# A routed expert stage: down weights in two buffers by parity, blank slots not gathered, router weights stationary in four column groups

## What is computed

```python
pg = softmax(xf @ w_rg); g_top = argmax(pg); pg_top = max(pg)
fl = (xf @ w_re) of the group g_top                   # 4 logits
top_p, top_i = top_k(softmax(fl), 2)
wts = top_p / sum(top_p) * pg_top
act = silu(xf @ w_gate[e]) * (xf @ w_up[e]) * comb[e] # comb: wts, 0 for experts not chosen
y = sum over e of act @ w_down[e]
```

## Time and profile before

| what | value |
|---|---|
| median of three runs | 2178.8 us (2172.47 to 2181.87) |
| profiled execution | 2173.51 us |
| its span, first to last instruction | 2171.4 us |
| PE busy | 1713.8 us, 79% |
| mean granted clock of TensorE | 0.831 |
| bytes by DMA | 375.76 MB |

### The profile page before, as it was taken

The page is one execution under the profiler, slowest core; times in us unless marked ns, Lnnn a source line. Parts: engine busy times, 40 slices in busy tenths (PEclk is TensorE's granted clock), DMA queues, the critical chain, the costliest instruction groups (busy, mean ns, idle before and its releaser), DMA issues. The chain is left out here.

```text
span 2171.4 us, 18914 instructions
## 1 busy us (share of the span) xinstructions
PE 1713.8 (79%) x7209; PEld 961.2 (44%) x7209; DVE 410.9 (19%) x828; ACT 283.2 (13%) x561; POOL 73.4 (3%) x96
## 2 busy tenths in 40 slices
PE   4699999937997588889769967786577878788781
PEld 2254444435555355677644435755323323233230
DVE  1110000031222343333340023112200000010104
ACT  1100000042221122222210011001000000000001
POOL 0000000000000000000000000000010010011010
PEclk9899999967997699855579979686687888798885
DMA  5354424043310445100052260027499699969984
GB/s 223 121 205 185 152 80 155 8 148 119 116 49 1 145 125 154 51 1 0 10 204 78 77 232 0 1 78 263 164 402 395 251 394 407 395 247 409 391 321 167
DMA packets 112001, 375.76 MB, mean 173 GB/s; under 512 B 18750, under 2 KB 46310, under 8 KB 82162
## 3 DMA queue, kind: packets, MB, share of 16 engines
q1 hardware_dynamic: 106258, 334.87, 40.8%
q0 software_dynamic: 5552, 31.99, 4.5%
q10 hardware_dynamic: 144, 8.26, 0.9%
HBM read 386.21 MB, written 26.49 MB: 190 GB/s over the span
## 5 line engine op out<-in xcount | busy, mean ns | idle before, releaser
L402 PE MATMUL bank<-w_in,hT 128*128 128x512 f32 (+1 forms) x640 | 259.1, 566 | 3.3 <-PEq L232 3.3
L1854 PE MATMUL bank<-w_g,hT_e 128*64 128x512 f32 x576 | 252.5, 597 | 0.9 <-DVE hT_e L1893 0.9
L1855 PE MATMUL bank<-w_u,hT_e 128*64 128x512 f32 x576 | 252.5, 597 | 0.0
L402 PEld LDWEIGHTS bank<-w_in,hT 128*128 128x128 f32 x640 | 117.2, 193 | 141.3 <-issue 141.3
L1871 PE MATMUL bank<-w_d,actT 128*64 128x512 f32 x576 | 166.1, 741 | 9.7 <-ACT actT L1882 9.7
L1854 PEld LDWEIGHTS bank<-w_g,hT_e 128*64 128x64 f32 x576 | 79.4, 138 | 167.3 <-issue 167.3
L747 PE MATMUL bank<-subT,w 128*128 128x504 f32 (+1 forms) x320 | 132.6, 545 | 0.0
L1844 PE MATMUL bank<-const,rows_in 64*128 64x64 f32 x304 | 38.0, 310 | 106.7 <-DMA rows_in<-scratch_hn,slot 106.7
L402 PE MATMUL bank<-w_out,mixT 128*128 128x512 f32 x256 | 112.4, 600 | 3.3 <-PEq L232 3.3
L1871 PEld LDWEIGHTS bank<-w_d,actT 128*64 128x64 f32 x576 | 48.8, 171 | 114.5 <-issue 114.5
L1844 PEld LDWEIGHTS bank<-const,rows_in 64*128 64x128 f32 x304 | 35.1, 201 | 122.1 <-issue 122.1
(11 more groups left out here) (353 smaller groups left out, 1856.5 us busy)
## 6 DMA issues: line engine op xcount, KB each, us to landing
w_g<-in_w_exp_gate SPq DMA_DIRECT2D x72, 1024.0 KB
w_u<-in_w_exp_up SPq DMA_DIRECT2D x72, 1024.0 KB
w_d<-in_w_exp_down SPq DMA_DIRECT2D x72, 1024.0 KB
w_in<-in_w_in SPq DMA_DIRECT2D x9, 4096.0 KB, 13.1
w_out<-in_w_out SPq DMA_DIRECT2D x4, 4096.0 KB
k_in<-in_cache_sel_k SPq DMA_DIRECT2D x64, 128.0 KB
v_in<-in_cache_sel_v SPq DMA_DIRECT2D x64, 128.0 KB, 2.3
w_mem<-in_w_mem_k SPq DMA_DIRECT2D x1, 4096.0 KB
```

Source lines behind the costliest of these rows:

```text
L402: mm = pe.matmul(bank[4 * u + r][:, 0:width], hT[:, c, r * P:(r + 1) * P], wbuf[u][:, c, 0:width], start=(c == 0), stop=(c == chunks - 1))
L1854: pe.matmul(bank[4 + u][0:NS, :], hT[:, u, c, :], w_g[:, c, :], start=(c == 0), stop=(c == KC - 1))
L1855: mm = pe.matmul(bank[4 + u][UP, :], hT[:, u, c, :], w_u[:, c, :], start=(c == 0), stop=(c == KC - 1))
```

## The change

It has four parts. (1) `w_d` gets two buffers, and turn t uses buffer t % 2. The loads of down for turn t wait for down of turn t-2, go ahead of the gate and up loads of that turn in SP's order, and are conditional on the expert of turn t-2. Down for turns 0 and 1 is loaded at the end of the norm. (2) From turn 2 on blank slots get an index out of bounds, and the gather checks bounds. (3) The router's logits are formed with the weights stationary, padded to 32 columns: chunk c goes to column group c % 4 and all 320 tokens stream; then the four partial sums are copied to SBUF and added by three matmuls with a constant. (4) To make room, the memory keys and values are freed before the stage, and the final stage uses the buffers of gate and up.

```diff
+        "lane_sum": np.where(p[:, None] % 32 == np.arange(20)[None, :], 1.0, 0.0),
...
                     def drain(i):
+                        rows = tiles[i][2].shape[-1]
...
-                                              bank[(i % 2) * 4 + j].rearrange("p (c r) -> p c r", c=4),
-                                              tiles[i][1][:, 4 * j:4 * j + 4].unsqueeze(2).to_broadcast([P, 4, P]),
+                                              bank[(i % 2) * 4 + j].rearrange("p (c r) -> p c r", c=4)[:, :, 0:rows],
+                                              tiles[i][1][:, 4 * j:4 * j + 4].unsqueeze(2).to_broadcast([P, 4, rows]),
...
-        w_d = sb(top, "w_d", [P, 4, D])
+        w_d = sb(top, "w_d", [P, 2, 4, D])
...
+        def down_loads(e, v):
+            d = A["w_exp_down"][0, bass.ds(e, 1)].rearrange("o (p c) n -> (o p) c n", c=4)
+            return [(w_d[:, v, q, :], d[:, q, :], d_loaded[v][q]) for q in range(4)]
...
-            w_r = sb(scope, "w_r", [P, KC, 20])
+            w_r = sb(scope, "w_r", [P, KC, 32])
+            part = sb(scope, "part", [P, TILES * P])
...
-                           last=[load for _, loads in expert_loads(0) for load in loads],
+                           last=[load for loads in gate_up_loads(0) for load in loads] + down_loads(0, 0) + down_loads(1, 1),
...
                     pe.wait_ge(wr_loaded, 32)
+                    pe.wait_ge(wr_padded, 1)
+                    for c in range(KC):
+                        lane = slice(32 * (c % 4), 32 * (c % 4) + 32)
+                        mm = pe.matmul(bank[3][lane, 0:SEQ + NS], w_r[:, c, :], hT[:, c, :], start=(c < 4), stop=(c >= KC - 4))
+                    mm.then_inc(parts_made, 1)
+                    pe.wait_ge(parts_kept, 1)
                     for r in range(TILES):
-                        for c in range(KC):
-                            mm = pe.matmul(bank[0][:, 20 * r:20 * r + 20], hT[:, c, r * P:(r + 1) * P], w_r[:, c, :],
-                                           start=(c == 0), stop=(c == KC - 1))
+                        mm = pe.matmul(bank[0][:, 20 * r:20 * r + 20], part[:, r * P:(r + 1) * P], cst("lane_sum"), start=True, stop=True)
...
+                    dve.memset(w_r[:, :, 20:32], 0.0).then_inc(wr_padded, 1)
+                    dve.memset(part[:, SEQ + NS:], 0.0)
+                    dve.wait_ge(parts_made, 1)
+                    dve.tensor_copy(part[:, 0:SEQ + NS], bank[3][:, 0:SEQ + NS]).then_inc(parts_kept, 1)
...
-                    dve.tensor_scalar(rows_at[:, :, 0], table[:, 0, :], -1.0, 0.0, ALU.add, ALU.max)
+                    dve.tensor_scalar(token_at[:, :], table[:, 0, :], -1.0, 0.0, ALU.add, ALU.max)
                     L(dve.tensor_scalar(blank[:, :], table[:, 1, :], 0.5, float(BLANK), ALU.is_lt, ALU.mult))
+                    dve.tensor_copy(rows_at[:, 0:2, 0], token_at[:, 0:2])
+                    dve.tensor_tensor(rows_at[:, 2:, 0], token_at[:, 2:], blank[:, 2:], ALU.add)
...
-                    with sp.Fori(1, n * 2) as turn:
-                        e = sp.value_load(experts[0:1, bass.ds(turn, 1)], min_val=0, max_val=NE - 1)
-                        before = sp.value_load(experts[0:1, bass.ds(turn - 1, 1)], min_val=0, max_val=NE - 1)
-                        for used, loads in expert_loads(e):
-                            sp.wait_ge(used, turn)
-                            for dst, src, loaded in loads:
-                                sp.dma_start(dst, src, cond=(e > before)).then_inc(loaded, 16)
+                    e, previous = expert_of(1), expert_of(0)
+                    for q, (dst, src, loaded) in enumerate(down_loads(e, 1)):
+                        sp.wait_ge(loaded, 16)
+                        sp.dma_start(dst, src, cond=(e < 1)).then_inc(loaded, 16)
+                    for q, loads in enumerate(gate_up_loads(e)):
+                        sp.wait_ge(gu_used[q], 1)
+                        for dst, src, loaded in loads:
+                            sp.dma_start(dst, src, cond=(e > previous)).then_inc(loaded, 16)
+                    with sp.Fori(1, n) as i:
+                        for u in range(2):
+                            turn = i * 2 + u
+                            e, previous, same_buffer = expert_of(turn), expert_of(turn - 1), expert_of(turn - 2)
+                            for q, (dst, src, loaded) in enumerate(down_loads(e, u)):
+                                sp.wait_ge(d_used[u][q], i)
+                                sp.dma_start(dst, src, cond=(e > same_buffer)).then_inc(loaded, 16)
+                            for q, loads in enumerate(gate_up_loads(e)):
+                                sp.wait_ge(gu_used[q], turn)
+                                for dst, src, loaded in loads:
+                                    sp.dma_start(dst, src, cond=(e > previous)).then_inc(loaded, 16)
...
-                                                in_offset=bass.IndirectOffsetOnAxis(ap=slot[0:NS, u, 0:1], axis=0)).then_inc(gathered[u], 16)
+                                                in_offset=bass.IndirectOffsetOnAxis(ap=slot[0:NS, u, 0:1], axis=0),
+                                                bounds_check=SEQ + NS - 1, oob_is_err=False).then_inc(gathered[u], 16)
...
-                            pe.wait_ge(d_loaded[q], turn * 16 + 16)
+                            pe.wait_ge(d_loaded[u][q], i * 16 + 16 + 16 * u)
...
-            y2 = sb(scope, "y2", [P, 2, TILES, D])
-            gf = sb(scope, "gf", [P, D])
-            junk = w_d[:, 0, :]
+            y2 = [w[:, :, :].rearrange("p (r c) f -> p r (c f)", r=4) for w in (w_g, w_u)]
+            gf = y2[0][:, 3, :]
+            junk = w_d[:, 0, 0, :]
```

More of the change, by code:

```diff
@@ L1603, in trunk, with gate_up_loads @@
         w_u = sb(top, "w_u", [P, KC, FF])
-        w_d = sb(top, "w_d", [P, 4, D])
-        gu_loaded, gu_used, d_loaded, d_used = ([sem(f"e_{n}{q}") for q in range(4)] for n in ("gu_loaded", "gu_used", "d_loaded", "d_used"))
-        def expert_loads(e):
+        w_d = sb(top, "w_d", [P, 2, 4, D])
+        gu_loaded, gu_used = ([sem(f"e_{n}{q}") for q in range(4)] for n in ("gu_loaded", "gu_used"))
+        d_loaded, d_used = ([[sem(f"e_{n}{v}{q}") for q in range(4)] for v in range(2)] for n in ("d_loaded", "d_used"))
+        def gate_up_loads(e):
             g = A["w_exp_gate"][0, bass.ds(e, 1)].rearrange("o (p c) f -> (o p) c f", c=KC)
             up = A["w_exp_up"][0, bass.ds(e, 1)].rearrange("o (p c) f -> (o p) c f", c=KC)
-            d = A["w_exp_down"][0, bass.ds(e, 1)].rearrange("o (p c) n -> (o p) c n", c=4)
             quarters = []
@@ L1867, in step @@
                         for q in range(4):
-                            pe.wait_ge(d_loaded[q], turn * 16 + 16)
+                            pe.wait_ge(d_loaded[u][q], i * 16 + 16 + 16 * u)
                             for n in range(4):
                                 lane = slice(NS * (n % 2), NS * (n % 2) + NS)
-                                mm = pe.matmul(bank[2 * u + n // 2][lane, :], actT[:, q, :], w_d[:, q, 512 * n:512 * n + 512], start=(q == 0), stop=(q == 3))
-                            mm.then_inc(d_used[q], 1)
+                                mm = pe.matmul(bank[2 * u + n // 2][lane, :], actT[:, q, :], w_d[:, u, q, 512 * n:512 * n + 512], start=(q == 0), stop=(q == 3))
+                            mm.then_inc(d_used[u][q], 1)
                     turns(pe, step)
@@ L1882, in step @@
                         act.copy(actT[:, :, :], bank[6][:, 0:4 * NS].rearrange("p (k r) -> p k r", k=4)).then_inc(a_copied, 1)
-                        act.wait_ge(d_used[3], turn + 1)
+                        act.wait_ge(d_used[u][3], i + 1)
                         act.wait_ge(y_stored, turn * 32)
@@ L1903, in step @@
                         drain(turn + 1, 1 - u)
-                        dve.wait_ge(d_used[3], turn + 1)
+                        dve.wait_ge(d_used[u][3], i + 1)
                         dve.wait_ge(y_stored, turn * 32)
@@ L1928, in _ @@
                             a = (k * TILES + r) * P
[L1929 removed]
+                            sp.dma_start(y2[k][0:rows, r, :], scratch["moe_y"][a:a + rows]).then_inc(y_loaded[r], 16)
                     for r in range(TILES):
@@ L1943, in add @@
                         dve.wait_ge(y_loaded[r], 32)
-                        own.link(dve.tensor_tensor(x[0:rows, r, :], x[0:rows, r, :], y2[0:rows, 0, r, :], ALU.add))
-                        dve.tensor_tensor(x[0:rows, r, :], x[0:rows, r, :], y2[0:rows, 1, r, :], ALU.add).then_inc(summed, 1)
+                        own.link(dve.tensor_tensor(x[0:rows, r, :], x[0:rows, r, :], y2[0][0:rows, r, :], ALU.add))
+                        dve.tensor_tensor(x[0:rows, r, :], x[0:rows, r, :], y2[1][0:rows, r, :], ALU.add).then_inc(summed, 1)
                     def finish(r):
```

22 lines of the change are left out of this document (13 added, 9 removed).

## The result

The changed kernel takes 2163.5 us (median of 8 executions, 2155.3 to 2171.8), the kernel before 2179.0 beside it (8 executions): a ratio of 0.9935, with an interval of 0.9909 to 0.9961. It is faster, by 14 us going by the ratio and 15.5 going by the medians, where 33 were forecast. Its profiled execution took 2168.26 us, with a span of 2166.4, and the granted clock is 0.835 in the mean.

The account below looks back on a forecast made before the run. Full turns were taken as bound equally by DMA time and the chain of scatter, gather, transposes and down. Terms -22.8, -7.0, +3.2, -3.5, +10.0, -13.6, +0.3 sum to -33.4, from 2178.8 to 2145.4 us, range 2124 to 2168.

Parts of the forecast that it names:

- 12 full turns: Expert turns that load weights: leaving out blank rows cuts each from 33.4 to 31.5 us, -22.8 in all.
- short turns 4 and 11: Turns that load nothing: a shorter gather cuts PE's wait and speeds down, 28.8 to about 25.3 us each, -7.0.
- turns 5 and 12: Turns after those that load nothing: their scatter meets down weights loaded a second time, making them full turns, +3.2 us.
- SP's hold: End of the norm: four more 1 MB loads issued there delay the router's start by 2.5 us each, +10.0.
- router: Router logits: four column groups running at once cut the stage from 20.7 to 7.1 us, -13.6.
- 3.5 us as fixed: Gather beside weight loads: 3.5 of 9.8 us taken as independent of rows, so leaving out blanks gives 7.0.
- 31.5, near the DMA end: Full-turn time chosen between bounds 30.6 and 33.4 us, guessing that many reads of one row halve the rate.
- 28.4 of 64: Blank slots taken per turn in the gathers: 1152 slots over 18 turns, 640 of them real.
- rival 2: Gathers: blank rows cost only their bytes, full turns give -6.6 us and short ones -4; total 2164.6, chance 0.18.
- Rival 3: Expert turns: PE's clock stays up, down takes 7.1 us and full turns 30.8; total 2133.6, chance 0.12.
- Rival 4: Expert stage: weight bytes alone bound it, 8.4 MB loaded twice cost 20 us, blanks save 0; total 2192, chance 0.04.
- Rival 5: Gathers: a skipped row costs as much as a read one in full and short turns; total 2175, chance 0.04.

Follow-up runs that it names:

- e7_wide: Kernel before, with each gathered row split into two 4 KB halves in 128 partitions instead of 8 KB in 64: 2180.9 us, ratio 1.0028.
- e1_spread: Kernel before, with each blank slot reading the token of its own partition number instead of token 0: 2177.1 us, ratio 1.0005.
- e9_early0: Kernel before, with the gather given its own index buffer so it no longer waits for the previous scatter: 2158.0 us, ratio 0.9920.
- e6_order: Changed kernel, with a turn's down loads behind its gate and up loads in SP's order: 2147.1 us, ratio 0.9867 to the kernel before.
- e10_all: Changed kernel, with expert loads issued in the router's block, down loads behind gate and up, and gathers not waiting for scatters: 2110.7 us, ratio 0.9717.
- e12_allwide: e10_all with each row gathered as two 4 KB halves into 128 partitions: 2095.8 us, ratio 0.9626.
- e4_parity: Kernel before, with only the two down buffers, SP's new order and sixteen loads ahead of the router: 2193.3 us, ratio 1.0088.
- e2_blanks: Kernel before, with only the blank slots left out of the gather from turn 2 on: 2156.5 us, ratio 0.9906.
- e5_loads: Changed kernel, with SP issuing the sixteen expert loads in the router's block, not at the norm's end: 2147.3 us, ratio 0.9865 to the kernel before.

## Why the prediction was wrong in size

The direction was right and the time lay inside the range, but less than half of the gain came. The forecast by its terms, in us, and what the two profiles show for each:

| term | forecast | found |
|---|---|---|
| 12 full turns | -22.8 | -11.9 |
| short turns 4 and 11 | -7.0 | -1.8 |
| turns 5 and 12 | +3.2 | +8.6 |
| last turn | -3.5 | -2.4 |
| SP's hold | +10.0 | +10.1 |
| router | -13.6 | -14.6 |
| the rest | +0.3 | +1.2 |
| sum | -33.4 | -10.8 |

**Blank slots: the step that failed.** This term was sized at 1.9 us for each full turn and measured 1.0. The prediction took "3.5 us as fixed" of a gather's 9.8 and let the other 6.3 shrink with the rows, so that the gather would fall by 2.8. It fell by 0.8 (from 9.4 to 8.5 in the table of e7_wide). A gather that meets weight loads takes 6.9 us for 4 rows, 7.7 for 20 and 9.8 for 64. By the last two a row costs 0.048 us, so 64 rows are 3.0 us and **6.8 us are fixed**, about twice what was assumed; a line through all 13 such gathers of the changed kernel gives 6.8 and 0.043. No row stood behind the 3.5. The earlier trace rows show 9.8 us with loads and 5.3 without, both for 64 rows, and the prediction let the whole difference shrink with the rows too. But most of it is a delay that a small transfer suffers beside large ones whatever its size, and leaving rows out doesn't take it away.

The choice of "31.5, near the DMA end" rested besides on many reads of one row, which e1_spread rules out, and on the transfers as the bound, which e7_wide and e9_early0 speak against: the chain is.

The even spread, "28.4 of 64" in every turn, was wrong too, but it cost the sum little: the gathers in the twelve full turns leave out 309 rows, 25.8 in the mean, which at the prediction's own price is 2 of the 22.8 us. What the spread does decide is where the gain lies. Six of these gathers read 44 rows or more and leave out 47 of 384 together; the pitches sum to 202.3 us where they took 201.1. The other six read 32 rows or fewer (20 in the mean), and their turns fell from 33.2 to 31.0 each, 13.1 us together. The spread could have been read from the trace of before: its scatters leave out blank lanes already, so the packets of q0 tell the real rows of each turn.

Of the prediction's own signs of being wrong two came: a window with a gather at 240 GB/s, near the 207, and turns 5 and 12 over 33 us.

The time is near rival 2's 2164.6, but that is luck: rival 2 had -6.6 for the full turns (found -11.9), +3.2 for turns 5 and 12 (+8.6) and -4 for the short turns (-1.8), and the differences nearly cancel. It was right that a blank row costs no more than a real one.

The Trainium skill (DMA: Bandwidth & Descriptors, "Anatomy of one DMA — SWDGE") gives 2 us plus bytes over 436 GB/s. For 20 and 64 rows that would be 2.4 and 3.2 us, a difference of 0.8. The runs show 7.7 and 9.8 beside weight loads: the fixed part is 3.4 times the page's, the price of a row 2.5 times. Here the measurement decides.

**Short turns.** "5.3 falls to about 3" was not far off: the gathers of 22 and 13 rows take 3.9 and 3.8 us to the transposes. But the turn fell by 0.7 and 1.1 instead of 3.5, since the other links of the chain stayed: down still takes 9.29 us in turn 4, at a granted clock of 0.76, though PE had stood for only 1.84 us before it. Of its own bounds, -1 and -4.5 a turn, the near one was right.

**Turns 5 and 12.** The mechanism was foreseen ("its scatter meets these loads"), and its size was not: the turn was said to become a full one of 31.5. A full one takes 33 to 34 (there are 64 rows to gather in turn 5), and these loads stand first in SP's order, just where the scatter starts. e6_order gives all of it back (58.3 us for the two, after 59.8 in the kernel before and 68.5 in the change). The old pitch of a full turn, 33.4, would have given +7.0 of the +8.6.

**SP's hold and the router** came out within 1 us each. Four more loads of 1 MB cost 10.1, at the transfers' own rate as in the earlier trace rows. Four column groups do run at once: 32 records of 320 columns take 4.22 us, where 4.5 was the estimate for four at once and 9.0 for two. The Trainium skill's four tiles of 128x32 (TensorEngine Tiling (Array Packing), "Available Configurations") say the same, and the trace agrees.

**The last turn** gained 2.4 of 3.5, within its bounds. That "a second down buffer removes no wait" was right, and the prediction did not carry it to its end: with no wait to remove, each load that it moves ahead could only cost.

**The other rivals.** Rival 3 (the clock stays up) did not come in the change: the granted clock over the turns is 0.86, after 0.84. It comes with the later edits, 0.93 in e10_all and 0.97 in e12_allwide, when PE waits far less. Rival 4 (every added byte paid) is out: e4_parity by itself does cost 19 us, but e6_order moves the same bytes in another order and its turns cost nothing for them. What e4_parity pays for is SP's hold and a late scatter. Rival 5 (a skipped row costs the same) is out: q0 moves 27.89 MB, and e2_blanks gains 20 us.

## What to carry to other kernels

When a chain and the transfers are equally long, first try what shortens the chain alone (here a wait of the gather that only a shared index buffer asked for): it shows which of the two is first, and how far behind the other lies. Split the time of a small transfer by its size before pricing what a smaller one saves: here two thirds of it were not the rows. An edit that makes transfers cheaper can be worth nothing or less before that, and 15 us after it. Count a load moved ahead by what it is put in front of: a block that ends with its issuing, or a small scatter on whose landing the next step waits.

## What the runs showed of the hardware

- A gather of 64 rows of 8 KB into 64 partitions goes with 207 to 260 GB/s for the whole core in the windows taken inside it, be its rows all different or in part one and the same. With the same bytes as 4 KB rows into 128 partitions it is 427. Which of the two matters, the size of a row or the number of partitions, wasn't tried; but the weight loads themselves are packets of 8 KB, into 128 partitions, and run at 420 alone. The Trainium skill (SBUF — State Buffer, "Door 1: The DMA port swizzle") says that a transfer's rate goes by how many of SBUF's 16 ports its partitions reach, and that 64 partitions reach no more of them than 32. The two rates point the same way, though they are not a test of it, as the size of a row changed too. That the loads beside such a gather slow down as well, the windows show.
- A small indirect transfer that meets 1 MB loads is late by a delay that hardly depends on its bytes. GpSimd's wait for the scatter is 3.6 us without them (e2_blanks, turn 5) and 7.2 beside them (e4_parity, the same turn). 20 gathered rows take 7.7 us to land and 4 rows 6.9, when 22 rows without loads take 3.8.
- A row left out of a gather by its index costs nothing that shows: q0 moves 27.89 MB where it moved 31.99, and the last gather, all of whose rows are blank, lands 2.1 us after its issue.
- SP can issue eleven loads of 1 MB at about 0.45 us each; from then on it stands for the transfers, and four more cost 10.1 us, 2.5 each (e4_parity and the change, 14.3 us where it was 4.3). Only a block that ends with the issuing has to pay for that: in e5_loads SP stands 15.74 us, and nobody waits.
